# Splitting the first six W_in blocks of an encoder layer into four parts instead of two, and two swaps of order in its last layer norm

## The chip, the cores and the metric

The kernel is written for one core of a Trainium2 chip: TensorE (matrix products), VectorE, ScalarE, GpSimd and SyncE, each with its own queue of instructions, an on-chip memory of 128 partitions, and eight accumulator banks of 128 x 512 fp32. It runs as one program on one core. The metric is the device time of one execution in microseconds (us). In the profile the engines are PE (with PEld for its weight loads), DVE (VectorE), ACT (ScalarE), POOL (GpSimd) and SP (SyncE).

## The reference

One layer of an encoder over two groups of 256 tokens (512 in all), D = 1024, fp32:

```python
mod = (silu(c) @ w_mod + b_mod)                  # shift1, scale1, gate1, shift2, scale2, gate2 per group
h = layer_norm(x) * (1 + scale1) + shift1
z = h @ w_in + b_in                              # (1024, 5120): u | v | p | gates
a = gelu(u) * (w_spatial @ ln(gelu(v)) + b)      # in chunks of 128 tokens, 8 heads
b = pool_scale * W_g(mean_window(p) - p)         # windows 2, 4, 8, 16
t = (sig(g_a) * (a @ w_branch_a) + sig(g_b) * (b @ w_branch_b)) @ w_out
x = ln(alpha * x + gate1 * t)
h = layer_norm(x) * (1 + scale2) + shift2
f = moe(h)                                       # 1 of 4 groups, 2 of its 8 experts, SwiGLU, 32 experts in all
y = ln(alpha * x + gate2 * f)
```

## The kernel before

**Split products.** Most products of the first half are made of three fast ones: each operand is held as hi (rounded to fp32r) plus lo (the rest), and hi x hi, hi x lo and lo x hi are summed in a bank. ScalarE makes the hi copy of a weight tile (`w_hi`), VectorE the lo (`w_lo`); the same for h (`h_hi`, `h_lo`). A "block" is 128 columns of W_in for all 512 tokens: 8 chunks (of 128 rows of W_in) x 3 products of 128 x 512. There are 56 blocks; the first eight are the v columns. W_in comes in units of 512 columns (four blocks, 2 MB), double buffered in `raw`.

**The start (to about 65 us).** The six first blocks (`FIRST = 6`) can't begin with whole chunks, since h needs the modulation: shift1 and scale1 come from c times 2048 columns of `w_mod` (8 MB). The 8 chunks of h are therefore cut into two parts of four (`PART`), and the matching columns of `w_mod` are loaded and multiplied part by part. The order is written out by hand for each queue:

- SP loads x (two transfers of 1 MB), then for each part eight transfers of 512 KB of `w_mod` and the W_in rows of that part for units 0 and 1 (lines 449 to 464). Then come sixteen transfers of 1 MB of the later modulation (`load_mod(8 + k)`; the buffer has two places, and load m waits for `pe_mod >= m - 1`), with W_in unit 2 in front of k = 3 (`load_unit`, which waits until block 3's split is done).
- TensorE: three `keep_clock` products (their result is not used), a modulation unit, transposes of the normalised x (`n_columns`, tiles of 128 tokens), and so on in turn; then the transposes of the scales (`first_mod_columns`), two more `keep_clock`s, and `part_pair(0)`: blocks 0 and 1 over part 0. Blocks 2 to 5 over part 0 follow, with the modulation units of part 1 between them, then `part_pair(1)`, then the loop over n (line 845) with block n over part 1, the transposes of the finished block n - 1, the transposes of `w_spatial` at n = 5, and one of the later modulation units at n = 1, 3, 5, 6, 7 (`mod_unit_at`). Six banks hold the six blocks open between the parts.
- ScalarE copies the transposed x to `n_t`, makes `w_hi` of the split blocks (`part_split_hi`) and half of the chunks of `h_hi` straight from `n_t`; the other half is copied from `h32`, which VectorE (`H_VECTOR`) and POOL (`H_POOL`) make.
- VectorE normalises x, adds the bias of the modulation (`first_mod_rows`), makes the scales (`first_scales`), `w_lo`, its share of `h32`, and `h_lo`.
- POOL, when the last `h_lo` is done (`dve_hlo >= KC`), issues the loads of `w_spatial`, `w_pool`, `b_spatial`, the router weights and biases (lines 578 to 587). TensorE's transposes at n = 5 wait for three of them.

**The middle.** The rest of W_in, the pools and gates, the two branches, W_out, the first layer norm and the routing follow, one block after the other on TensorE. The 32 experts (192 MB of weights) are loaded from the end of block 56 on.

**The end.** For four tiles i of 128 tokens the last layer norm adds three terms: `second_added(i)` and `based(i)` on VectorE put alpha x and two expert rows together (in a pair of banks, with a sum for the mean), TensorE adds the rows of the last two experts (`last_rows`), `base_means` and `means` make the means, ScalarE sums the squares (`deviation(i)`), VectorE applies mean and gain (`centred_gain`), makes the inverse deviation (`inverse`), and the scaled rows go out through ScalarE and POOL (`scaled`, tiles 0 and 1) or VectorE (`scaled_bias`, tiles 2 and 3). Tile 3's first step is done in halves (`based_half`).

Of the kernel before, what the change touches and what calls it, by code (L numbers as in the profile page):

```python
# [36 lines left out]
PART = KC // 2  # L37
H_DIRECT = (0, 1, 4, 5)
H_VECTOR = (3, 0, 7, 4)
H_POOL = (2, 1, 6, 5)  # L40


def hybrid_encoder(nc, x_prompt, x_sample, c_prompt, c_sample, w_mod, b_mod, w_in, b_in, w_spatial,
# [12 lines left out]
    with ctx:  # L56
# [5 lines left out]
        def sem(name):  # L62
# [20 lines left out]
        modraw0 = [at(f"modraw0_{i}", [128, 2, 2, 512], f32, o)  # L83
                   for i, o in enumerate([2 * SLOT + 8 * K * j for j in range(4)] + [32 * K, 40 * K] + [SLOT + 32 * K, SLOT + 40 * K])]
# [42 lines left out]
        modrow_first = at("modrow_first", [128, 2, 512], f32, S0 + 9728 + 4096)  # L127
# [259 lines left out]
        def first_mod_source(part, kc):  # L387
            return w_mod[0, 128 * kc:128 * kc + 128, 0:2048].rearrange("p (v f n) -> p v f n", v=2, f=2)[:, :, part, :]

        def halves_of_chunks(tiles, turn):  # L390

            first = PART * (turn // 2 % 2)
            return tiles[turn % 2][:, first:first + PART, :]

# [163 lines left out]
        def _(pool):  # L558
# [4 lines left out]
            for v in range(2):  # L563
                for r in range(REQ):
                    pool.dma_start(modrow_first[64 * v + r:64 * v + r + 1, :, :],
                                   b_mod[0:1, 1024 * v:1024 * v + 1024].rearrange("a (f n) -> a f n", f=2)).then_inc(s_bmod, 16)
# [4 lines left out]
            for kc in H_POOL:  # L571
# [142 lines left out]
        def _(pe):  # L714
# [15 lines left out]
            def first_mod_unit(part, q):  # L730
                if part == 0:
                    pe.wait_ge(s_m0[q], 32)
                else:
                    pe.wait_ge(s_m0[4 + q // 2], 64)
                for k in range(2):
                    for v in range(2):
                        j = 2 * v + k
                        x = mm(MOD[32 * j:32 * j + 32, :], silu_c[:, 2 * q + k, :], modraw0[4 * part + q][:, k, v, :], start=(q == 0), stop=(q == 3))
                x.then_inc(pe_mod, 1)

            def first_mod_columns(part):
                pe.wait_ge(dve_row0, part + 1)
                for k in range(4):
# [3 lines left out]
            for _ in range(3):  # L747
                keep_clock(512)
            pe.wait_ge(act_pro, 1)

            def n_columns(i):
                pe.wait_ge(dve_n, i + 1)
                if i >= 2:
                    pe.wait_ge(act_nt, 2 * (i - 1))
                for kc in range(KC):
                    bank = B[2 * (i % 2) + kc // 4]
                    x = pe.transpose(bank[:, 128 * (kc % 4):128 * (kc % 4) + 128], xin[:, i, 128 * kc:128 * kc + 128], ident)
# [12 lines left out]
            pe.wait_ge(dve_pro, 1)  # L770
            first_mod_columns(0)
            keep_clock(512)
            keep_clock(256)

            def block_at(b, i, mov_hi, mov_lo, freed, count):
                pe.wait_ge(act_whi, FIRST + b + 1)
                pe.wait_ge(dve_wlo, FIRST + b + 1)
# [8 lines left out]
            def part_split(part, b):  # L786
                turn = FIRST * part + b
                pe.wait_ge(act_whi, turn + 1)
                pe.wait_ge(dve_wlo, turn + 1)
                return bank_of(b), halves_of_chunks(w_hi, turn), halves_of_chunks(w_lo, turn)  # L790

            def part_pair(part):
                for k in range(PART):
                    kc = PART * part + k
                    pe.wait_ge(act_hhi, kc + 1)
                    for b in range(2):
                        if k == 0:
                            part_split(part, b)
                        hi, lo = (halves_of_chunks(w, FIRST * part + b) for w in (w_hi, w_lo))
                        mm(bank_of(b)[:, :], hi[:, k, :], h_hi[:, kc, :], start=(kc == 0), stop=False)  # L800
                        mm(bank_of(b)[:, :], lo[:, k, :], h_hi[:, kc, :], start=False, stop=False)
                for k in range(PART):
                    kc = PART * part + k
                    pe.wait_ge(dve_hlo, kc + 1)
                    for b in range(2):
                        x = mm(bank_of(b)[:, :], halves_of_chunks(w_hi, FIRST * part + b)[:, k, :], h_lo[:, kc, :], start=False, stop=(kc == KC - 1))
                        if k == PART - 1:
                            x.then_inc(pe_blk if part else pe_part, 1)

            def part_block(part, b):  # L810
# [6 lines left out]
                x.then_inc(pe_blk if part else pe_part, 1)  # L817
# [27 lines left out]
            for n in range(8):  # L845
                if 2 <= n < FIRST:
                    part_block(1, n)
# [1696 lines left out]
```

## Time and profile before

| | |
|---|---|
| three runs | 943.0, 945.49, 944.63 us, median 944.63 |
| profiled execution | 942.63 us, its span 940.9 us |
| granted TensorE clock, mean | 0.991 |
| PE busy | 897.1 us (95%), 4420 products |
| DVE, ACT, POOL busy | 381.0, 243.1, 118.1 us |
| moved by DMA | 295.32 MB, mean 314 GB/s |

Busy times are sums over the span. A product's duration in the trace is longer than the step from one product to the next, since they are pipelined. A row of the timeline gives start, duration, engine, line and operation, the tiles written and read, how many instructions it merges, and in brackets the idle time in front of it with what ended it. Most products have line 716, that of a helper; they are told apart by their tiles (`modraw,silu_c` is a modulation unit, `cst` a keep_clock).

### The profile page before, as it was taken

Reading aid. Unit: us, or ns where it says so; the run is one execution under the profiler, and the core shown is the slowest. Engines: PE = TensorE matmul, PEld = TensorE weight load, DVE = VectorE, ACT = ScalarE, POOL = GpSimd, SP = SyncE. Lnnn points to the kernel's source line nnn. Section 1 sums busy time; section 2 is a strip of 40 time slices with the busy share of each in tenths; the row PEclk is TensorE's granted clock in tenths of the full one; section 3 lists DMA queues with packets and bytes.
Section 4 is the critical chain, followed back from the end, with each engine's and each line's share of the span. In section 5 each row is a group of like instructions: output and inputs, shape, how many; then the busy total and the mean of one; then the engine's idle time right before and its main releaser. Section 6 shows DMA issues by size and latency. Waiting matters only on the chain. (4 is left out here: it accounts for less than half of the span.)

```text
span 940.9 us, 12139 instructions
## 1 busy us (share of the span) xinstructions
PE 897.1 (95%) x4420; PEld 547.3 (58%) x4420; DVE 381.0 (40%) x657; ACT 243.1 (26%) x360; POOL 118.1 (13%) x149
## 2 busy tenths in 40 slices
PE   5999999999999999999999999998998999999894
PEld 2677767888888888787544444444444344444331
DVE  5543434565344236798622322222122132321346
ACT  3342335331333225446410111011011101110113
POOL 3130556000001000000000000000000100000041
PEclk9999999999999999999999999999999999999997
DMA  9975676274665623908999999999999999999993
GB/s 341 363 246 191 224 269 224 90 267 179 222 225 153 183 90 101 300 1 367 399 384 419 427 426 426 426 427 427 429 426 425 424 387 428 429 427 427 422 412 122
DMA packets 51291, 295.32 MB, mean 314 GB/s; under 512 B 5438, under 2 KB 6558, under 8 KB 35986
## 3 DMA queue, kind: packets, MB, share of 16 engines
q1 hardware_dynamic: 40784, 263.47, 69.9%
q0 software_dynamic: 9952, 29.80, 9.4%
q10 hardware_dynamic: 482, 1.13, 0.3%
q8 instruction: 39, 0.64, 0.3%
q14 instruction: 34, 0.28, 0.1%
HBM read 275.81 MB, written 22.83 MB: 317 GB/s over the span
## 5 line engine op out<-in xcount | busy, mean ns | idle before, releaser
L716 PE MATMUL banks<-down_w,hid_t 128*64 128x512 f32 x512 | 119.7, 610 | 11.9 <-issue 10.9
L716 PE MATMUL banks<-h_hi,w_hi 128*128 128x512 f32 x320 | 125.0, 391 | 0.5 <-ACT h_hi L1398 0.5
L716 PE MATMUL banks<-h_lo,w_hi 128*128 128x512 f32 x320 | 125.2, 398 | 0.0
L716 PE MATMUL banks<-h_hi,w_lo 128*128 128x512 f32 x320 | 124.8, 390 | 0.0
L716 PE MATMUL banks<-up_w,x_by_expert 128*64 128x512 f32 x256 | 112.6, 593 | 0.0
L716 PE MATMUL banks<-gate_w,x_by_expert 128*64 128x512 f32 x256 | 112.5, 592 | 0.0
L716 PE MATMUL banks<-up_w,x_by_pair 128*64 128x512 f32 x240 | 105.4, 592 | 0.0
L716 PE MATMUL banks<-gate_w,x_by_pair 128*64 128x512 f32 x240 | 105.4, 592 | 0.0
L1615 ACT ACTIVATE sg_hid<-banks 64x512 f32<-64x512 f32 x33 | 19.5, 592 | 313.8 <-PE banks L716 313.8
L2177 DVE TENSOR_TENSOR sg_hid<-banks,sg_hid 64x512 f32<-64x512 f32 x32 | 22.2, 694 | 177.9 <-ACT sg_hid L1615 177.9
L685 POOL DMA_INDIRECT round_y<-yout,store_row x30 | 31.0, 1034 | 461.5 <-DVE yout L2300 448.7
L1806 DVE TENSOR_TENSOR w_lo<-raw,w_hi 128x1024 fp32r<-128x1024 f32 x50 | 61.4, 1228 | 67.0 <-ACT w_hi L1353 66.9
L716 PEld LDWEIGHTS banks<-down_w,hid_t 128*64 128x64 f32 x512 | 36.3, 140 | 72.2 <-issue 65.2
L716 PEld LDWEIGHTS banks<-gate_w,x_by_expert 128*64 128x64 f32 x256 | 34.9, 137 | 70.8 <-issue 70.7
L1353 ACT ACTIVATE w_hi<-raw 128x1024 fp32r<-128x1024 f32 (+1 forms) x62 | 59.8, 970 | 61.2 <-PE banks L716 54.3
L716 PEld LDWEIGHTS banks<-h_lo,w_hi 128*128 128x128 f32 x320 | 60.1, 188 | 25.1 <-issue 8.4
L716 PEld LDWEIGHTS banks<-gate_w,x_by_pair 128*64 128x64 f32 x240 | 32.9, 137 | 66.5 <-issue 66.5
L716 PE MATMUL banks<-sel_group,h_hi 128*128 128x256 f32 x256 | 69.7, 306 | 0.0
L2300 DVE TENSOR_TENSOR yout<-banks,yout 128x512 f32<-128x512 f32 x32 | 22.1, 691 | 112.9 <-PE banks L716 112.8
L716 PEld LDWEIGHTS banks<-h_hi,w_hi 128*128 128x128 f32 x320 | 60.2, 188 | 12.7 <-ACT h_hi L1398 1.1
L716 PEld LDWEIGHTS banks<-h_hi,w_lo 128*128 128x128 f32 x320 | 60.1, 188 | 12.7
L716 PE MATMUL banks<-sel_group,h_lo 128*128 128x256 f32 x256 | 63.6, 282 | 1.4 <-issue 1.4
(331 smaller groups left out, 1314.7 us busy)
## 6 DMA issues: line engine op xcount, KB each, us to landing
down_w<-in_w_exp_down SPq DMA_DIRECT2D x29, 2048.0 KB, 20.5
gate_w<-in_w_exp_gate SPq DMA_DIRECT2D x28, 2048.0 KB, 18.5
up_w<-in_w_exp_up SPq DMA_DIRECT2D x28, 2048.0 KB, 22.9
modraw<-in_w_mod SPq DMA_DIRECT2D x16, 1024.0 KB, 4.9
raw<-in_w_in SPq DMA_DIRECT2D x8, 2048.0 KB, 9.7
round_y<-zrow POOLq DMA_DIRECT2D x6, 2048.0 KB, 7.6
modraw<-in_w_mod SPq DMA_DIRECT2D x16, 512.0 KB, 11.4
down_w<-in_w_exp_down SPq DMA_DIRECT2D x6, 1024.0 KB, 14.8
```

What stands on the lines that cost most here:

```text
L685: pool.indirect_dma_start(round_halves, bass.IndirectOffsetOnAxis(store_row[:, e:e + 1], 0), yout[s][:, :], None, bounds_check=2 * LAST_RO ...
L716: return pe.matmul(out, lhsT, rhs, start=start, stop=stop, skip_group_check=True)
L1353: return act.activation(out, in_, ACT.Copy, scale=scale)
L1615: act.activation(sgb[0:CAP, :], bank[0:CAP, :], ACT.Silu).then_inc(sm["silu"], 1)
L1806: dve.tensor_tensor(w_lo[par][:, :, :], raw[:, u % 2, :, 128 * (b % 4):128 * (b % 4) + 128], w_hi[par][:, :, :].bitcast(f32), ALU.subtract ...
L2177: dve.tensor_tensor(sg_hid[CAP:128, :], B[0][CAP:128, :], sg_hid[0:CAP, :], ALU.mult).then_inc(m_sem["hid"], 1)
L2300: dve.tensor_tensor(yout[s][:, :], B[1][:, :], yout[s][:, :], ALU.mult).then_inc(m_sem["yo"], 1)
```

## The change

**Start.** The parts are four of two chunks. A part needs 256 columns of shift and of scale, so its eight modulation transfers are of 256 KB (pieces of 1 KB) instead of 512 KB; there are 32 instead of 16. The W_in rows of a part are two chunks. Of unit 1 only half the columns are loaded with part 0, the others behind part 1. TensorE has one `keep_clock` of 512 columns at first and one of 256 behind the first two modulation units; those around the first scales go. The transposes of x are done in halves: the first four chunks of all tiles ahead of the first scales, the last four of tiles 1 to 3 between the scales' transposes and the first products, and ScalarE copies their results between the splits of part 0. All of `h_hi` comes straight from `n_t` on ScalarE; VectorE makes the even chunks of `h32`, POOL the odd. The loads of the later modulation wait for all eight units of the first (`pe_mod >= 8`).

**End.** VectorE does tile 3's add ahead of the means, ScalarE tile 2's squares ahead of tile 0's scaled rows.

The core of the diff:

```diff
-PART = KC // 2
-H_DIRECT = (0, 1, 4, 5)
-H_VECTOR = (3, 0, 7, 4)
-H_POOL = (2, 1, 6, 5)
+NPART = 4
+PART = KC // NPART
+WIDE = 128 * PART
+BEFORE = FIRST * (NPART - 1)
...
 # SP
-                    sp.wait_ge(dve_wlo, FIRST + 4 * (u - 1))
+                    sp.wait_ge(dve_wlo, BEFORE + 4 * (u - 1))
...
-                sp.wait_ge(pe_mod, m - 1)
+                sp.wait_ge(pe_mod, max(KC, m - 1))
...
-            for part in range(2):
+            for part in range(NPART):
                 for kc in range(KC):
-                    m = 4 * part + kc // 2
-                    landed = s_m0[4 + kc // 4 if part else kc // 2]
-                    sp.dma_start(modraw0[m][:, kc % 2, :, :], first_mod_source(part, kc)).then_inc(landed, 16)
+                    landed = s_m0[part + 1 if part else kc // 4]
+                    sp.dma_start(modraw0[part][kc // 2][:, kc % 2, :, :], first_mod_source(part, kc)).then_inc(landed, 16)
                 chunks = slice(PART * part, PART * part + PART)
                 if part == 0:
                     for c in range(2):
                         cols = slice(256 * c, 256 * c + 256)
                         sp.dma_start(raw[:, 0, chunks, cols], unit_source(0)[:, chunks, cols]).then_inc(s_wpre[c], 16)
-                    sp.dma_start(raw[:, 1, chunks, :], unit_source(1)[:, chunks, :]).then_inc(s_wpre[2], 16)
+                    sp.dma_start(raw[:, 1, chunks, 0:256], unit_source(1)[:, chunks, 0:256]).then_inc(s_wpre[1], 16)
                 else:
                     for u in range(2):
-                        sp.dma_start(raw[:, u, chunks, :], unit_source(u)[:, chunks, :]).then_inc(s_w[u], 16)
+                        landed = {1: s_m0[5], 2: s_wpre[2], 3: s_w[u]}[part]
+                        sp.dma_start(raw[:, u, chunks, :], unit_source(u)[:, chunks, :]).then_inc(landed, 16)
+                if part == 1:
+                    sp.dma_start(raw[:, 1, 0:PART, 256:512], unit_source(1)[:, 0:PART, 256:512]).then_inc(s_m0[5], 16)
...
 # TensorE
-            for _ in range(3):
-                keep_clock(512)
+            keep_clock(512)
             pe.wait_ge(act_pro, 1)
...
-            first_mod_unit(0, 0)
-            n_columns(0)
-            n_columns(1)
-            first_mod_unit(0, 1)
-            n_columns(2)
-            n_columns(3)
-            first_mod_unit(0, 2)
-            first_mod_unit(0, 3)
+            first_mod_units(0, 0, 2)
             keep_clock(256)
-            pe.wait_ge(act_nt, 2 * TILES)
+            n_columns(0, 0)
+            n_columns(0, 1)
+            n_columns(1, 0)
+            first_mod_units(0, 2, 4)
+            n_columns(2, 0)
+            n_columns(3, 0)
             pe.wait_ge(dve_pro, 1)
             first_mod_columns(0)
-            keep_clock(512)
-            keep_clock(256)
+            for i in range(1, TILES):
+                n_columns(i, 1)
...
-            part_pair(0)
-            first_mod_unit(1, 0)
-            part_block(0, 2)
-            first_mod_unit(1, 1)
-            part_block(0, 3)
-            first_mod_unit(1, 2)
-            first_mod_unit(1, 3)
-            part_block(0, 4)
-            pe.wait_ge(dve_col, 1)
-            first_mod_columns(1)
-            part_block(0, 5)
-            part_pair(1)
+            for part in range(NPART - 1):
+                part_pair(part)
+                part_block(part, 2)
+                first_mod_units(part + 1, 0, 4)
+                part_block(part, 3)
+                first_mod_columns(part + 1)
+                part_block(part, 4)
+                part_block(part, 5)
+            part_pair(NPART - 1)
             for n in range(8):
                 if 2 <= n < FIRST:
-                    part_block(1, n)
+                    part_block(NPART - 1, n)
...
 # ScalarE
             for i in range(TILES):
...
+                n_copied(i, 0)
             part_split_hi(0, 0)
             part_split_hi(0, 1)
+            act.wait_ge(act_nt, TILES)
             h_high(0)
-            for b in range(2, FIRST):
-                part_split_hi(0, b)
-            part_split_hi(1, 0)
-            part_split_hi(1, 1)
-            h_high(1)
+            part_split_hi(0, 2)
+            n_copied(0, 1)
+            n_copied(1, 1)
+            part_split_hi(0, 3)
+            n_copied(2, 1)
+            n_copied(3, 1)
+            part_split_hi(0, 4)
+            part_split_hi(0, 5)
+            act.wait_ge(act_nt, 2 * TILES)
+            for part in range(1, NPART):
+                part_split_hi(part, 0)
+                part_split_hi(part, 1)
+                h_high(part)
+                if part < NPART - 1:
+                    for b in range(2, FIRST):
+                        part_split_hi(part, b)
...
             deviation(1)
+            deviation(2)
             scaled(0)
-            deviation(2)
             scaled(1)
...
 # VectorE
+            for part in range(NPART):
+                first_mod_rows(part)
+                part_split_lo(part, 0)
+                if part:
+                    part_split_lo(part, 1)
+                first_scales(part)
+                dve.wait_ge(dve_col, 2 * part + 2)
+                if part == 0:
+                    part_split_lo(part, 1)
+                elif part == 2:
+                    dve.wait_ge(act_nt, 2 * TILES)
+                modulated(PART * part)
+                for kc in range(PART * part, PART * part + PART):
+                    h_low(kc)
+                if part < NPART - 1:
+                    for b in range(2, FIRST):
+                        part_split_lo(part, b)
...
             based(2)
+            second_added(3)
             base_means(0, 3)
             means()
-            second_added(3)
             dve.wait_ge(f_open, 3)
```

`first_mod_units(part, first, last)` does the units first to last of a part with 256 columns each (four products a unit, on four strips of 32 columns of the array), and `n_columns(i, hb)` four transposes of tile i instead of eight.

## Rows read from the trace of the kernel before

**Rows 1.** Windows by stage: busy us (instructions) per engine, granted clock, DMA share, GB/s.

```profile
100.00:200.00 100.00, 99.70 (x469) 74.07 (x462) 46.02 (x65) 44.13 (x62) 38.69 (x49) 1.00 0.57 208
400.00:920.00 520.00, 502.34 (x2565) 245.56 (x2563) 178.08 (x366) 91.26 (x156) 41.97 (x42) 0.99 0.95 398
```

**Rows 2.** Timeline of TensorE at the start (start, duration in us): keep_clock products.

```profile
10.37 5.49 PE L716 MATMUL banks<-cst 128*128 128x512 f32 x6
...
25.20 1.46 PE L716 MATMUL banks<-cst 128*128 128x512 f32 x4
```

**Rows 3.** The same timeline, from the first product of the blocks on.

```profile
27.16 0.50 PE L716 MATMUL banks<-h_hi,w_hi 128*128 128x512 f32 x1 [0.51 <-ACT h_hi L1398]
...
40.47 0.39 PE L716 MATMUL banks<-h_hi,w_lo 128*128 128x512 f32 x1
40.78 1.92 PE L716 MATMUL banks<-modraw,silu_c 128*32 128x512 f32 x16
...
42.98 0.40 PE L716 MATMUL banks<-h_hi,w_hi 128*128 128x512 f32 x1
...
52.36 1.98 PE L716 MATMUL banks<-h_lo,w_hi 128*128 128x512 f32 x8
54.89 0.66 PE L825 MATMUL banks<-cst,g 128*128 128x128 f32 x4 [0.55 <-ACT g L1432]
```

**Rows 4.** Timeline of the POOL and SP queues, 50 to 80 us: loads issued.

```profile
51.90 0.99 POOL L579 DMA_DIRECT2D ws_raw<-in_w_spatial  x1 [2.64 <-DVE h_lo L1840]
...
56.60 0.33 SPq L447 DMA_DIRECT2D modraw<-in_w_mod  x1
...
64.20 15.90 SPq L447 DMA_DIRECT2D modraw<-in_w_mod  x3
```

**Rows 5.** DMA issues at 56.60 and 64.20: KB, us to landing.

```profile
modraw<-in_w_mod SPq DMA_DIRECT2D x1, 1024.0 KB, 11.3
...
modraw<-in_w_mod SPq DMA_DIRECT2D x1, 1024.0 KB, 12.2
```

**Rows 6.** Timeline of VectorE at the end.

```profile
921.13 0.16 DVE L2425 SCALAR_TENSOR_TENSOR fin<-banks,fin 128x4 f32<-128x4 f32 x1 [1.08 <-PE banks L716]
921.21 1.28 DVE L2322 SCALAR_TENSOR_TENSOR y_second<-y_second,route_w,res 128x1024 f32<-128x1024 f32 x1
...
923.66 1.28 DVE L2445 SCALAR_TENSOR_TENSOR y_first<-banks,fin,ln_bc 128x1024 f32<-128x1024 f32 x1
...
929.08 1.29 DVE L2445 SCALAR_TENSOR_TENSOR banks<-banks,fin,ln_bc 128x1024 f32<-128x1024 f32 x1 [0.59 <-ACT squares L1720]
```

**Rows 7.** Timeline of the SP queue, the first loads.

```profile
1.89 9.28 SPq L455 DMA_DIRECT2D modraw<-in_w_mod  x8
11.22 4.05 SPq L460 DMA_DIRECT2D raw<-in_w_in  x2
```

**Rows 8.** DMA issue at 1.89 (KB, us to landing), and the window 20 to 21.

```profile
modraw<-in_w_mod SPq DMA_DIRECT2D x1, 512.0 KB, 9.4
...
20.00:21.00 1.00, 1.00 (x10) 1.00 (x11) 0.00 (x0) 0.23 (x1) 0.00 (x0) 1.00 1.09 353
```

**Rows 9.** Timeline of TensorE, transposes of w_spatial and modulation unit 3.

```profile
70.57 1.04 PE L855 MATMUL banks<-cst,ws_raw 128*128 128x128 f32 x8
...
78.64 1.06 PE L716 MATMUL banks<-modraw,silu_c 128*32 128x512 f32 x8
```

**Rows 10.** Timeline of ScalarE at the start.

```profile
18.16 2.06 ACT L1353 ACTIVATE n_t<-banks 128x512 f32<-128x512 f32 x4 [5.16 <-PE banks L757]
...
26.02 2.08 ACT L1398 ACTIVATE h_hi<-n_t,mod_t,scale1p 128x256 fp32r<-128x256 f32 x4 [1.86 <-DVE scale1p L1825]
```

**Rows 11.** Timeline of ScalarE at the end.

```profile
926.71 1.15 ACT L1353 ACTIVATE y_second<-y_first,fin 128x1024 f32<-128x1024 f32 x1 [1.43 <-DVE fin L2454]
927.77 1.09 ACT L1720 ACTIVATE squares<-banks,fin 128x1024 f32<-128x1024 f32 x1
```

**Rows 12.** Timeline of TensorE at the end.

```profile
922.51 2.85 PE L716 MATMUL banks<-yout,last_t 64*128 64x512 f32 x12
```

More of the change, by code:

```diff
@@ L387, in first_mod_source, with part_of_chunks @@
         def first_mod_source(part, kc):
-            return w_mod[0, 128 * kc:128 * kc + 128, 0:2048].rearrange("p (v f n) -> p v f n", v=2, f=2)[:, :, part, :]
-        def halves_of_chunks(tiles, turn):
-            first = PART * (turn // 2 % 2)
+            return w_mod[0, 128 * kc:128 * kc + 128, 0:2048].rearrange("p (v f n) -> p v f n", v=2, f=NPART)[:, :, part, :]
+        def part_of_chunks(tiles, turn):
+            first = PART * (turn // 2 % NPART)
             return tiles[turn % 2][:, first:first + PART, :]
@@ L728, in keep_clock, with first_mod_units @@
                 mm(B[4][:, 0:w], ident, cst[:, 0:w])
-            def first_mod_unit(part, q):
+            def first_mod_units(part, first, last):
                 if part == 0:
-                    pe.wait_ge(s_m0[q], 32)
+                    pe.wait_ge(s_m0[first // 2], 64)
                 else:
[L734 to L739, printed above, removed]
+                    pe.wait_ge(s_m0[part + 1], 128)
+                for q in range(first, last):
+                    for k in range(2):
+                        for v in range(2):
+                            j = 2 * v + k
+                            x = mm(MOD[32 * j:32 * j + 32, 0:WIDE], silu_c[:, 2 * q + k, :], modraw0[part][q][:, k, v, :], start=(q == 0), stop=(q == 3))
+                    if q % 2 == 1:
+                        x.then_inc(pe_mod, 1)
@@ L762, in _, with n_columns @@
-            n_columns(1)
-            first_mod_unit(0, 1)
-            n_columns(2)
-            n_columns(3)
-            first_mod_unit(0, 2)
-            first_mod_unit(0, 3)
-            keep_clock(256)
-            pe.wait_ge(act_nt, 2 * TILES)
+            def n_columns(i, hb):
+                bank = B[i if hb == 0 else (4, 5, 0, 1)[i]]
+                if hb == 0:
+                    pe.wait_ge(dve_n, i + 1)
+                elif i >= 2:
+                    pe.wait_ge(act_nt, i - 1)
+                for k in range(4):
+                    first = 512 * hb + 128 * k
+                    x = pe.transpose(bank[:, 128 * k:128 * k + 128], xin[:, i, first:first + 128], ident)
+                x.then_inc(pe_xt, 1)
@@ L805, in part_pair @@
                     for b in range(2):
-                        x = mm(bank_of(b)[:, :], halves_of_chunks(w_hi, FIRST * part + b)[:, k, :], h_lo[:, kc, :], start=False, stop=(kc == KC - 1))
+                        x = mm(bank_of(b)[:, :], part_of_chunks(w_hi, FIRST * part + b)[:, k, :], h_lo[:, kc, :], start=False, stop=(kc == KC - 1))
                         if k == PART - 1:
-                            x.then_inc(pe_blk if part else pe_part, 1)
+                            x.then_inc(pe_blk if part == NPART - 1 else pe_part, 1)
             def part_block(part, b):
@@ L816, in part_block @@
                     x = mm(bank[:, :], lo[:, k, :], h_hi[:, kc, :], start=False, stop=(kc == KC - 1))
-                x.then_inc(pe_blk if part else pe_part, 1)
+                x.then_inc(pe_blk if part == NPART - 1 else pe_part, 1)
             def transposes(k, zs, trs):
@@ new lines, in n_copied, with h_high @@
+            def n_copied(i, hb):
+                act.wait_ge(pe_xt, ((1, 3, 4, 5), (2, 6, 7, 8))[hb][i])
+                copy(n_t[:, 4 * hb:4 * hb + 4, 128 * i:128 * i + 128],
+                     B[i if hb == 0 else (4, 5, 0, 1)[i]][:, :].rearrange("p (k n) -> p k n", k=4)).then_inc(act_nt, 1)
+            def h_high(part):
+                act.wait_ge(dve_col, 2 * part + 2)
+                for kc in range(PART * part, PART * part + PART):
+                    for r in range(REQ):
+                        x = act.activation(h_hi[:, kc, SEQ * r:SEQ * r + SEQ], n_t[:, kc, SEQ * r:SEQ * r + SEQ], ACT.Identity,
+                                           scale=scale1p[:, kc, r:r + 1], bias=mod_t[:, 0, kc, r:r + 1])
+                    x.then_inc(act_hhi, 1)
```

115 lines of the change are left out of this document (37 added, 78 removed).

## The prediction

> **What bounds the kernel now.** I read the busy time by stage first: in 100 to 200 us TensorE works 99.70 of 100 us, and the experts' stage (400 to 920 us) runs at a DMA share of 0.95 from loads that start only when the last W_in block is done [rows 1]. So any time won or lost before 100 us, if it is not given back there, comes out at the end. Then I read TensorE's own timeline of the start: 27.16 us pass before the first product of real work, which waits for ScalarE's h_hi, and from there products follow each other nearly without a gap to 54.34, where the second pair ends, and after 0.55 us of waiting for the first GELU on through the blocks [rows 2, 3]. Last, the transfers: the loads that the later steps of this stage wait for are issued by SP and POOL when TensorE and VectorE reach certain points [rows 4, 5]. At the end VectorE is the chain: it stands idle 1.08 us before the means and 0.59 us before tile 2's gain [rows 6].
>
> The profiled execution took 942.63 us (span 940.9, 1.7 around it); the median of the runs shown is 944.63. I work out a difference on the profile and put it on the median.
>
> **When the first product starts.** The first 512 KB of modulation weights landed 9.4 us after their issue at 1.89, at 11.3 [rows 7, 8]. While 1 KB pieces passed (the two half loads of the first W_in unit) the queues moved 353 GB/s [rows 8]. 512 KB are 1.5 us at that rate, so the weights of a part begin to land at about 9.8; the first half of part 0 (1.05 MB) is there at 12.8, the second at 15.8, where the old part 0 needed 4.2 MB, to about 21.7. TensorE: one keep_clock of 512 columns instead of three, two records of 0.915 [rows 2], ends at 12.2. Two mod units, 256 columns wide: 1.7 us at that pace, 0.9 at the later one (three 512-column equivalents in 1.46, so 0.49 a record [rows 2]). Then keep_clock(256), 12 transposes at 0.13 (8 took 1.04 [rows 9]) or twice that, two units, 8 transposes. At the full pace from 15.5 on this ends at 18.9, at half pace throughout at 22.0. ScalarE then has one more n_t copy (4 took 2.06 [rows 10]), a split of 256 columns (about 0.35), VectorE its own (0.4) and the scales (0.6), ScalarE the first h_hi (two of 0.52 [rows 10]): 3.1 us. First product at 22.0 or 25.2. The pace changed somewhere between 15.9 and 25.2 before [rows 2]; I take 23.0, **4.2 us earlier** than 27.16. The 12 transposes of the second n_t halves (1.6 us) lie in front of the pair, but beside the scales and h_hi, so they cost nothing.
>
> **What the four parts cost on TensorE.** A product follows the last by 0.227 us (eight took 1.98, the last lasting 0.39 [rows 3]). Two 512-column mod units cost 42.98 - 40.47 - 2 x 0.227 = 2.06 us [rows 3]; four 256-column units have the same columns. Two transposes of scales: 0.26. A part is 36 products, the units and the transposes of the next: 8.17 + 2.06 + 0.26 = 10.5 us. Three parts and the last pair (12 products, 2.72): the pair ends 34.5 us after the first product, at 57.5 instead of 54.34. Behind it 24 products are left instead of 48, 5.46 us less. TensorE alone would thus be at mod unit 3 (the fourth of the later ones, in block 6) at 57.5 + (78.64 - 54.34) - 5.46 = 76.3, against 78.64 [rows 9]: **2.3 us won**. The 4.2 won at the start pay 1.9 for two more sets of units and transposes and shorter waits.
>
> The other engines keep up: in part 0 ScalarE has six splits (2.1), h_hi (2.1) and four n_t copies (2.1) for 10.5 us of products; each later part less. All of part 3's modulation weights have landed at 9.8 us + 11.55 MB / 353 GB/s = 42.5 (four times 2.10 MB, the W_in pieces of the first three parts 3.15), and are needed 25.2 after the first product, at 48.2. The waits added (act_nt before the banks of part 0, pe_part before a w place is used again) are for things done at least 2 us before; queued behind them is only the same block.
>
> **What is late next.** Mod units 2 and 3 of the later modulation need loads that can't be issued earlier: load 10 waits for unit 0, which stands behind the last pair; W_in unit 2 waits for block 3's split; load 11 stands behind it on SP. POOL's eight loads wait for the last h_lo. All of them come later, not earlier, because the last pair ends later: the last scales are transposed 28.6 us after the first product, and 1.1 for the scales, 2.1 for two chunks of h_hi and 0.7 for h_lo put h_lo's end at 55.5 instead of 51.6 (+3.9; POOL's first issue was 51.90 [rows 4]), load 10 from 56.60 to 59.8 (+3.2). And they are slow there: load 10 took 11.3 us, load 11 12.2, for 1 MB each [rows 5], and the queues are full from POOL's first load on. Load 11 landed at 64.20 + 12.2 = 76.4, 2.2 before its unit at 78.64 [rows 4, 5, 9]. Now its unit would be ready at 76.3, and the load lands 3.2 to 3.9 later than before: I take 3.4, 79.8. The stall is 3.5 us, spread over units 2 and 3, and unit 3 starts **1.2 us later** than before (bounds: 2.3 earlier with no stall, 1.7 later with the full 3.9). From there the loads and needs are as before. That is where the expected gain goes.
>
> **The tail.** Tile 3's add (1.28 us at 921.21) fills the 1.08 us idle ahead of the means [rows 6]; the means go 0.3 later, to 921.4. TensorE is busy until 922.08 anyhow. The next half product of tile 3 then starts a microsecond earlier, but tile 0's gain waits for the squares of tile 0, which follow the means (end 922.9 instead of 922.5): from 923.66 to 922.9, 0.75 us won. On ScalarE tile 2's squares ran at 927.77, behind the scaled rows of tile 0 at 926.71 [rows 11], though TensorE had finished tile 2 at 922.51 + 2.85 = 925.36 [rows 12]. Moved ahead they run at 925.4 and are through at 926.9, just as the scaled rows become ready. VectorE's 0.59 us of waiting before 929.08 goes too: 929.08 - 0.59 - 0.75 = 927.75. What follows is one chain on VectorE to the end; tile 3's squares come at 929.1, in time. **1.25 us won** (0.7 if the squares still come last, 1.4 at most). POOL's adds of tiles 0 and 1 go at most 0.3 later, and end 1.3 before tile 3's rows.
>
> **Sum:** +1.2 - 1.25 = 0: 942.6 by the profile, 944.6 on the median.
>
> **Rivals.**
> A. The loads keep up (POOL's loads, with the queues free of load 10 a little longer, end sooner): no stall, 2.3 + 1.25 = 3.55 won, 941.1. For it: the 2.2 us of slack that load 11 had. Against: the queues were full then, and both triggers move later. Chance 0.18.
> B. TensorE's pace stays at half through the start, since two keep_clocks ahead of it and two behind go and 1 us of idle comes in at 12.2: first product at 25.2, everything in the stage 2.2 later, +2.1: 946.7. For it: the six records of 0.915 at 10.37 [rows 2], where steady work had not yet raised the pace. Against: from 12.8 on the work is close to gapless, and before, with TensorE at work since 10, the granted clock was 1.00 (the upper level, 2.4 GHz) at 20 to 21 [rows 8]. Chance 0.14. The Trainium skill (TensorE: Matmul & The Clock Gate, Part 1) says that the slow clock is the default and that activity releases it; by that rule what matters is how gapless the new start is, and by it the 25.2 would be the upper end. The pace in [rows 2] agrees with two levels a factor of two apart.
> C. The slower one: 1 KB pieces pass at the pace of their issue, 2.0 us for 512 KB in the first W_in unit, 262 GB/s [rows 7]. Place: the modulation weights of the parts. Of the 11.55 MB 9.45 are in 1 KB pieces, so part 3's land at 9.8 + 9.45 / 0.262 + 2.1 / 0.353 = 51.8, TensorE waits at each part, the last pair ends at 51.8 + 9.3 = 61.1 (+6.7), load 11 lands at 83.1: +4.5 - 1.25 = +3.3, 947.9. It decides from about 290 GB/s down, and from 270 it is slower by more than 0.3%. Against it: the 353 GB/s while such pieces moved. Chance 0.10. [...]
>
> **Chances.** My forecast 0.55, A 0.18, B 0.14, C 0.10, else 0.03. A measurement of this kernel tells about 0.3% (2.8 us) from no change. Faster: A and a little of the forecast, 0.22. Slower: C and the upper part of B, 0.16. Same 0.62. Range 940.8 to 948.0: A at the one end, C at the other.
>
> **What would show it.** First product at 22 to 24 us; the last pair of the split blocks ending near 57; two DMA waits on TensorE, before mod units 2 and 3, of some 3.5 us together, and unit 3 at 79 to 80. No idle on VectorE before tile 2's gain, and the tail shorter by about 1.2. Wrong if unit 3 runs near 76 with no wait (A), if the first product comes after 25 (B), or if TensorE waits for modulation weights inside the parts (C).

## The result, and the profile after

The changed kernel takes 948.83 us (median of 20 runs, 944.7 to 952.54) against 944.68 (20 runs, 942.05 to 946.11) for the kernel before beside it: ratio 1.0047, 95% interval 1.0035 to 1.0058. It is slower by 4.2 us. The prediction had 944.6, no difference, and a range that ended at 948.0. The profiled execution spans 944.9 us against 940.9.

TensorE's timeline of the start in the changed kernel (start and duration in us, what it did, the idle time just ahead):

```profile
13.40 1.94 PE L719 MATMUL banks<-modraw,silu_c 128*32 128x256 f32 x16 [0.96 <-DMA modraw<-in_w_mod]
...
23.33 0.50 PE L719 MATMUL banks<-h_hi,w_hi 128*128 128x512 f32 x1 [1.63 <-ACT h_hi L1405]
...
27.71 1.93 PE L719 MATMUL banks<-modraw,silu_c 128*32 128x256 f32 x32
...
38.23 1.93 PE L719 MATMUL banks<-modraw,silu_c 128*32 128x256 f32 x32
...
48.74 1.93 PE L719 MATMUL banks<-modraw,silu_c 128*32 128x256 f32 x32
...
58.51 0.66 PE L834 MATMUL banks<-cst,g 128*128 128x128 f32 x4 [0.55 <-ACT g L1447]
```

The first product of real work comes 3.8 us earlier than before (27.16 in [rows 3]), the parts follow each other in 10.5 us without a wait for weights, and the transposes behind the last pair come at 58.51 instead of 54.89. All of this is as predicted, within 0.5 us. The size of the gain differs between profiles: the first product comes at 26.16 to 27.24 us in the four profiles with the start of before (before, e1, e13, e14) and at 23.13 to 24.48 in the eight whose start up to there is that of the changed kernel. Then the same engine, further on: the transposes of w_spatial, mod units 2 and 3 with the products behind unit 3, and unit 4 (units are counted from 0; load 8 + k feeds unit k):

```profile
69.52 1.09 PE L861 MATMUL banks<-cst,ws_raw 128*128 128x128 f32 x8 [0.67 <-DMA bs_bc<-in_b_spatial]
71.50 1.06 PE L719 MATMUL banks<-modraw,silu_c 128*32 128x512 f32 x8 [0.89 <-DMA modraw<-in_w_mod]
...
81.62 1.70 PE L719 MATMUL banks<-modraw,silu_c 128*32 128x512 f32 x8 [2.94 <-DMA modraw<-in_w_mod]
83.25 0.80 PE L719 MATMUL banks<-h_lo,w_hi 128*128 128x512 f32 x1
83.84 0.63 PE L719 MATMUL banks<-h_hi,w_hi 128*128 128x512 f32 x1
...
90.31 1.06 PE L719 MATMUL banks<-modraw,silu_c 128*32 128x512 f32 x8
```

Three waits for transfers, 4.50 us together, where [rows 9] had none; and the unit behind the longest takes 1.70 us instead of 1.06, the products 0.63 instead of 0.39. The windows there (busy time of PE, PEld, DVE, ACT, POOL; granted clock; DMA share; GB/s) show the clock at its lower level, 0.50, that is 1.2 GHz, after 2.9 us in which TensorE stood still, though it was busy throughout those 2 us:

```profile
82.00:84.00 2.00, 2.00 (x10) 0.66 (x3) 0.00 (x0) 0.00 (x0) 0.00 (x0) 0.50 0.21 86
84.00:86.00 2.00, 2.00 (x8) 1.59 (x7) 0.00 (x0) 0.00 (x0) 0.00 (x0) 0.67 0.81 209
```

From mod unit 3 to mod unit 4 it takes 8.69 us; before, 85.74 - 78.64 = 7.10. Unit 3 is 3.0 us later than before, unit 4 4.57. The loads behind it, on the queues of GpSimd and SyncE and as transfers (KB, us to landing; the two transfers are loads 10 and 11):

```profile
56.30 0.99 POOL L582 DMA_DIRECT2D ws_raw<-in_w_spatial  x1 [1.85 <-DVE h_lo L1852]
...
60.22 0.33 SPq L448 DMA_DIRECT2D modraw<-in_w_mod  x1
60.59 0.62 SPq L444 DMA_DIRECT2D raw<-in_w_in  x1
65.07 0.33 SPq L448 DMA_DIRECT2D modraw<-in_w_mod  x1
...
modraw<-in_w_mod SPq DMA_DIRECT2D x1, 1024.0 KB, 11.2
...
modraw<-in_w_mod SPq DMA_DIRECT2D x1, 1024.0 KB, 16.5
```

Load 11 is issued 0.9 us later than in [rows 4] but takes 16.5 us instead of 12.2 [rows 5]. From there on little is given back: the stages of [rows 1] read nearly the same,

```profile
100.00:200.00 100.00, 99.87 (x471) 74.04 (x470) 43.41 (x59) 41.00 (x58) 39.02 (x51) 1.00 0.58 208
400.00:920.00 520.00, 504.99 (x2569) 248.27 (x2569) 176.39 (x368) 92.83 (x156) 42.25 (x42) 0.99 0.95 396
```

the first expert's gate weights are issued at 384.96 instead of 380.43 (+4.53), and expert 31's down product starts at 917.96 instead of 913.87 (+4.09). The end is measured from there. VectorE's timeline answers to [rows 6], SyncE's shows the output stores:

```profile
925.44 0.16 DVE L2434 SCALAR_TENSOR_TENSOR fin<-banks,fin 128x4 f32<-128x4 f32 x1
...
931.87 1.28 DVE L2454 SCALAR_TENSOR_TENSOR banks<-banks,fin,ln_bc 128x1024 f32<-128x1024 f32 x1
...
937.27 1.28 DVE L2468 SCALAR_TENSOR_TENSOR y_second<-banks,fin,ln_bc 128x1024 f32<-128x1024 f32 x1
...
934.64 0.56 SPq L554 DMA_DIRECT2D out<-y_second  x1
935.24 0.58 SPq L556 DMA_DIRECT2D out<-y_second  x1
935.87 4.19 SPq L554 DMA_DIRECT2D out<-y_second  x3
```

Both idle times of [rows 6] are gone, and VectorE is through 20.59 us after 917.96, where before it was 21.70 after 913.87: 1.1 won. But the span ends 26.94 after it, before 27.03: 0.1 won. Behind VectorE's last instruction 6.35 us pass instead of 5.33. Tile 3's store on SyncE's queue, before and then in the changed kernel, makes up most of that: it starts 0.03 us behind VectorE's end before, 0.19 now, and takes 1.32 us to issue instead of 0.47.

```profile
935.60 0.47 SPq L551 DMA_DIRECT2D out<-y_second  x1
```

```profile
938.74 1.32 SPq L554 DMA_DIRECT2D out<-y_second  x1
```

### The profile page after: what moved, and what is told of

Same layout as the page of the kernel before. It is cut to its first block and busy times, and to the rows that moved or that the text cites. A ratio compares the mean times of both kernels' runs of the same rounds, so it can differ in the third digit from the quotient of the medians.

```text
span 944.9 us, 12332 instructions
## 1 busy us (share of the span) xinstructions
PE 897.2 (95%) x4476; PEld 549.2 (58%) x4476; DVE 382.4 (40%) x677; ACT 246.7 (26%) x376; POOL 118.3 (13%) x149
## 5 line engine op out<-in xcount | busy, mean ns | idle before, releaser
L719 PE MATMUL banks<-down_w,hid_t 128*64 128x512 f32 x512 | 122.0, 620 | 10.8 <-issue 8.9
L719 PEld LDWEIGHTS banks<-h_lo,w_hi 128*128 128x128 f32 x320 | 60.3, 189 | 24.5 <-issue 10.3
## 6 DMA issues: line engine op xcount, KB each, us to landing
down_w<-in_w_exp_down SPq DMA_DIRECT2D x6, 1024.0 KB, 10.8
```

The source lines that it names most:

```text
L719: return pe.matmul(out, lhsT, rhs, start=start, stop=stop, skip_group_check=True)
```

## The experiments

**Theory**: the parts do what they should; the loss is the late loads of 56 to 82 us, the lower clock behind the wait, and output stores that crowd. **Rivals**: the parts themselves cost it, the waits only show it; or the exchanges at the end do. Read from each profile are the first real product, mod unit 4 (a mark behind all the start's waits), VectorE's end and the span's end behind the start of expert 31's down product, and the median with its ratio to the kernel before on the same chip. Each mark is read from one profile; the medians are of 5 to 20 runs, but e5 and e8 were run once and have no ratio. The kernel before took 942.99 to 944.68 us in these groups; e1, e13 and e14 have its start, e2 and e8 that of the changed kernel.

| kernel | first product | mod unit 4 | VectorE's end | span's end | median us | ratio (95%) |
|---|---|---|---|---|---|---|
| before | 27.16 | 85.74 | 21.70 | 27.03 | 944.68 | 1 |
| changed | 23.33 | 90.31 | 20.59 | 26.94 | 948.83 | 1.0047 (1.0035-1.0058) |
| e1 tail alone | 26.16 | 85.64 | 20.06 | 27.06 | 944.13 | 1.0005 (0.9989-1.0020) |
| e2 start alone | 24.41 | 91.57 | 21.90 | 26.68 | 948.38 | 1.0048 (1.0033-1.0064) |
| e3 load 11 first | 24.26 | 88.71 | 20.69 | 27.21 | 944.97 | 1.0008 (0.9990-1.0026) |
| e4 third place | 24.48 | 87.14 | 21.71 | 28.41 | 944.22 | 0.9995 (0.9979-1.0012) |
| e5 busy through the wait | 23.13 | 88.81 | 20.29 | 26.95 | 946.76 | one run |
| e6 + ws, wp, bs early | 24.10 | 85.51 | 20.59 | 26.80 | 944.10 | 1.0004 (0.9989-1.0020) |
| e7 + product at the start | 22.33 | 83.15 | 20.84 | 27.14 | 942.25 | 0.9986 (0.9971-1.0001) |
| e12 (e7 again) | 21.98 | 82.63 | 21.56 | 28.28 | 942.33 | 0.9982 (0.9963-1.0000) |
| e11 (e7, add alone) | 22.29 | 83.06 | 20.97 | 25.91 | 939.36 | 0.9955 (0.9937-0.9974) |
| e8 fewer stores | 23.14 | 88.58 | 21.83 | 26.91 | 946.43 | one run |
| e9 ws, wp, bs early alone | 24.06 | 86.34 | 21.41 | 28.16 | 944.13 | 1.0002 (0.9979-1.0026) |
| e10 (e9 + product) | 22.77 | 86.08 | 20.63 | 27.07 | 942.39 | 0.9979 (0.9960-0.9998) |
| e13 before + add | 27.24 | 85.83 | 20.76 | 26.19 | 942.61 | 0.9979 (0.9964-0.9994) |
| e14 before + squares | 27.05 | 85.67 | 21.02 | 27.61 | 944.02 | 0.9994 (0.9978-1.0010) |

**e1, e2: each half of the change alone.** e1 is the kernel before with the two exchanges at the end (the last hunk under ScalarE and the last under VectorE), e2 the changed kernel without them.

> The kernel before with the two exchanges at the end alone (tile 3's add ahead of the means, tile 2's squares ahead of tile 0's scaled rows). Theory (the loads of the start and the output stores decide): VectorE's last instruction ends about 20.6 us after main_down(31) instead of 21.7, but the last two output stores then stand behind the others, so the time moves by -0.3 to +0.2 us: about 944.6. As the prediction had it: -1.25 us, 943.4. Rival (the tail itself costs, since tile 0's rows are scaled later): slower by 0.5 us or more, 945.2 or above.

> The changed kernel with the old order at the end: the four parts alone. Theory: the whole loss is the start's, so about +4.1 us on before (948.8), and the mod unit 4 of the first loop still starts 4.6 us later than before (90.3 against 85.74). Rival (part of the loss is the tail's): 948.0 or less. If the prediction's tail gain of 1.25 us had been real at the end: 950.

The whole loss is the start's: e2's interval (five runs) is nearly that of the changed kernel, e1's takes in 1. VectorE ends earlier in e1, and the span's end does not move.

**e3: load 11 ahead of W_in unit 2.**

```diff
-                if k in (3, 8, 12):
-                    load_unit(k // 4 + (2 if k == 3 else 1))
+                if k in (8, 12):
+                    load_unit(k // 4 + 1)
                 load_mod(8 + k)
+                if k == 3:
+                    load_unit(2)
```

> The changed kernel, with W_mod's load 11 issued ahead of the 2 MB load of W_in unit 2 on SyncE's queue, nothing else. Theory (mod unit 3 waits for load 11, which shares the transfer engines with unit 2 and with GpSimd's loads): load 11 is issued at about 65 us as now, but lands at 75 to 77 instead of 81.6; the wait of 2.94 us before mod unit 3 goes, the unit takes 1.06 instead of 1.70 us, the products after it keep 0.23 us spacing, and mod unit 4 starts at 85.8 instead of 90.3: about -4.5 us, 944.3. W_in unit 2 lands at 80 to 84, before block 8 wants it. Rival (the parts themselves cost it: the blocks' work of part 3 ends 3.6 us later, and the wait only shows it): another wait takes its place, mod unit 4 stays at 89 or later, 947.5 or more.

The wait before unit 3 is gone, load 11 taking 10.6 us instead of 16.5, and the ratio falls from 1.0047 to 1.0008: by the time the rival falls. By the mark it is close: mod unit 4 comes at 88.71, where 85.8 was expected and the rival had 89 or later. The first product is 0.9 later, and another wait costs clock: behind 0.84 us for bs and 1.16 for load 10, 2 us apart, unit 2 takes 1.50 us, the window behind it shows

```profile
74.00:76.00 2.00, 2.00 (x8) 1.41 (x5) 0.00 (x0) 0.00 (x0) 0.00 (x0) 0.50 1.02 377
```

and unit 3 follows in 8.72 us instead of 7.1.

**e4: a third place for the loads of W_mod.** It keeps e3's order of load 11 and W_in unit 2.

```diff
-        modraw = at("modraw", [128, 2, 4, 512], f32, SLOT + 32 * K)
+        modraw = [at(f"modraw{j}", [128, 4, 512], f32, o) for j, o in enumerate((SLOT + 32 * K, SLOT + 40 * K, 20 * K))]
...
-            for k in range(16):
+            for k in (2, 0, 1, *range(3, 16)):
```

> The changed kernel with a third place in SBUF for W_mod's loads: load 10 needs no place of an earlier one and is issued ahead of loads 8 and 9, into the 5 us in which the transfer engines now stand still (46 to 51 us); load 11 takes load 8's place (issued at about 60 instead of 65 us) and goes ahead of W_in unit 2. Theory: no wait for W_mod is left (0.89 and 2.94 us gone), perhaps 0.3 to 0.7 us for GpSimd's last load remains; mod unit 4 starts at 84.2 to 85 us instead of 90.3 (before: 85.74): -5.4 to -6.1 us on the changed kernel, 942.8 to 943.4, 1 to 2 us under the kernel before. Rival (the parts themselves cost it): not under 946.

The stretch that it is to fill, in the changed kernel (DMA share and GB/s at the end of the line):

```profile
46.00:51.00 5.00, 5.00 (x47) 3.29 (x46) 1.08 (x4) 0.54 (x2) 0.00 (x0) 1.00 0.00 0
```

No wait for loads 10 and 11 is left, and the ratio is 0.9995. The 942.8 to 943.4 us expected did not come (944.22), nor did unit 4 at 84.2 to 85 (87.14): the first product is 1.15 later than in the changed kernel, and bs, which GpSimd issues last of its large loads, is now what TensorE waits for, 1.89 us instead of the 0.3 to 0.7 expected:

```profile
71.88 1.09 PE L869 MATMUL banks<-cst,ws_raw 128*128 128x128 f32 x8 [1.89 <-DMA bs_bc<-in_b_spatial]
```

**e5: TensorE kept busy through the wait.** Its one run took 946.76 us.

```diff
+                if n == 6:
+                    for _ in range(3):
+                        mm(COL[:, 0:512], ident, cst[:, 0:512])
```

> The changed kernel with three more 128x512 products of the identity into a free bank just ahead of mod unit 3, where TensorE now waits 2.94 us (some 2.2 us of work at the full level). Theory (the wait itself is the load's, but behind it TensorE runs at 1.2 GHz for some 3.5 us because it stood still, and this costs 1.6 us more): unit 3 starts no earlier against the first product, the unit takes 1.06 us, the products behind it keep 0.23 us spacing, and the distance from mod unit 3 to mod unit 4 is 7.1 us instead of 8.69. Rival (the slow products after the wait have another cause, as the arriving transfers): the distance stays at 8.7 us, or grows.

```profile
77.80 2.74 PE L719 MATMUL banks<-cst 128*128 128x512 f32 x6
81.70 1.06 PE L719 MATMUL banks<-modraw,silu_c 128*32 128x512 f32 x8 [1.16 <-DMA modraw<-in_w_mod]
...
88.81 1.06 PE L719 MATMUL banks<-modraw,silu_c 128*32 128x512 f32 x8
```

The wait ends at the same time, the load being no earlier, but unit 4 follows in 7.11 us: 1.6 us of the loss were the clock's, paid behind the wait and not in it. e8, which has the changed kernel's start unaltered, shows the same by chance: there bs was late, TensorE waited 2.62 us for it and only 0.50 for load 11, the clock fell at the first of the two (0.50 at 72 to 74 us), and from unit 3 to unit 4 it took 7.10.

**e6, e9: GpSimd's loads earlier**, on the third place (e6) and alone on the changed kernel (e9).

```diff
             for kc in range(1, KC, 2):
+                if kc == KC - 1:
+                    pool.wait_ge(dve_hlo, 3 * PART)
+                    pool.dma_start(ws_raw[:, :, :], ...)
+                    ...
```

> The kernel with a third place for W_mod's loads, and GpSimd's loads of ws, wp and bs issued ahead of its last modulated block, behind h_lo of part 2 (at about 45.5 us instead of 56.3), so that they move in the 5 us in which the transfer engines stand still. Theory: the wait of 1.89 us for bs before the transposes of ws goes, no wait of TensorE for a transfer is left between 56 and 90 us; mod unit 4 starts 60.7 us behind the first real product (62.7 without this step, 67.0 in the changed kernel): about -1.9 us against the third place alone, 942.3, some 1.5 us under the kernel before. Rival (these loads only collide with load 10 and loads 8 and 9 instead): mod unit 0 or 1 waits, and the time stays at 944 or more.

> The changed kernel with GpSimd's loads of ws, wp and bs (2 MB) issued behind h_lo of part 2, at about 45.5 us, and nothing else: two places for W_mod's loads and their order as in the changed kernel. Theory (the late loads are late because five transfers share the engines after 56 us): load 10, W_in unit 2 and load 11 have the engines nearly to themselves, 4 MB from 60.2 us at the 400 GB/s that the profile shows is 10.5 us, so load 11 is there by 71 to 73, and no wait for it or for bs is left; mod unit 4 starts 60.7 to 61.5 us behind the first real product (67.0 in the changed kernel): about 943 to 944, the same as with the third place as well. Rival (it is the late issue of load 11 and unit 2 ahead of it that matter, not GpSimd's loads): a wait of 1.5 us or more before mod unit 3 stays, 946 or more.

bs is no longer waited for in either, and in e9 nothing waits before units 1 to 4, with the two places and the order of the changed kernel. So what made load 11 late was GpSimd's 2 MB and the 2 MB of W_in unit 2 together: taking either out of its way is enough (e9, e3). What these loads now run into is what e6's rival said and the two theories missed: loads 8 and 9 took a median of 10.8 us in e6 and 11.4 in e9, against 5.8 in the changed kernel, mod unit 0 waits 0.76 and 1.65 us, and e6 took 944.10 us where its theory had 942.3. On the whole time e6 and e9 are no better than e4.

**e7, e10, e12: one more product at the start**, `keep_clock(256)` behind `keep_clock(512)`; e7 and e12 are one kernel, on e6, e10 is on e9.

> The kernel of the run before with one more 128x256 product of the identity ahead of the first mod unit, into the 0.9 to 1.3 us in which TensorE waits for W_mod's first pieces. Theory (that idle microsecond puts off the step to 2.4 GHz, which came at about 16 us in one profile of the changed start and at 18 to 19 in three others, with the first real product at 23.3 and 24.3 to 24.5): the step comes by 15 us, and the first real product starts at 22.0 to 23.3: -1.0 to -2.4 us, about 941. Rival (the first product hangs on the transfers or on ScalarE's rows, not on TensorE's level): it stays at 23.3 or later, the time as the run before.

> The run before (loads of ws, wp and bs earlier) with one more 128x256 product of the identity ahead of the first mod unit. Theory: first real product at 22.3 us as in the run with the third place and this product, the time about 942, no different from that run's; the third place is then not needed. Rival: mod unit 2 or 3 waits for its load by 1 us or more, since TensorE gets there 1 to 2 us earlier; 943.5 or more.

> The kernel with the third place, the earlier loads and the one more product at the start, once more, beside the kernels that it is to be compared with. Expected as the first time: 942.3 us, 0.1 to 0.2% under the kernel before, mod unit 4 at 83.2 to 84 us.

```profile
10.44 2.93 PE L728 MATMUL banks<-cst 128*128 128x512 f32 x4
13.31 1.53 PE L728 MATMUL banks<-modraw,silu_c 128*32 128x256 f32 x16
14.78 0.70 PE L728 MATMUL banks<-cst 128*128 128x256 f32 x2
15.31 1.47 PE L776 MATMUL banks<-cst,xin 128*128 128x128 f32 x12
```

This is e12. The mod units at 13.31 are already faster than the 1.94 of the changed kernel, the 12 transposes take 1.47 us where e2, e3, e4, e6 and e9 show 2.54 to 2.77, and the first real product comes at 21.98 to 22.77 in all four profiles with the extra product, against 23.13 to 24.48 in the eight profiles without it; the granted clock rises at 13.8 to 16.0 us in the four and at 16.5 to 19.4 in the eight. With it and the third place the start is at last ahead of before: mod unit 4 at 82.6 to 83.2 instead of 85.74. In e10, without the third place, unit 0 waits 1.15 us (0.05 to 0.21 in e7, e11 and e12), the clock falls (0.56 at 62 to 64 us), and unit 4 comes at 86.08, though the time of the whole can't be told from e7's. The fall does not follow from the length of the wait: e9 waited 1.65 us at the same place and kept the clock. Units 0 and 1 in e10, then in e9:

```profile
59.73 1.36 PE L720 MATMUL banks<-modraw,silu_c 128*32 128x512 f32 x8 [1.15 <-DMA modraw<-in_w_mod]
...
66.13 1.07 PE L720 MATMUL banks<-modraw,silu_c 128*32 128x512 f32 x8
```

```profile
61.54 1.07 PE L720 MATMUL banks<-modraw,silu_c 128*32 128x512 f32 x8 [1.65 <-DMA modraw<-in_w_mod]
...
66.38 1.06 PE L720 MATMUL banks<-modraw,silu_c 128*32 128x512 f32 x8
```

**e8: fewer stores.** Its one run took 946.43 us.

> The changed kernel, which leaves out the two output stores of tile 1 (that quarter of the output is not written), so that nothing is queued between the stores of tile 2 and tile 3. Theory (the 1.1 us that VectorE wins at the end are lost because the stores crowd): the stores of tile 3 are issued in 0.5 us instead of 1.32, and the span ends 5.3 us or less behind VectorE's last instruction instead of 6.35. Rival (the end hangs on tile 3's own stores, whatever else is stored): it stays 6.2 to 6.5 us.

The span ends 5.08 us after VectorE's last instruction: the theory's 5.3 or less. Tile 3's store is issued in 0.51 us, as expected:

```profile
939.65 0.51 SPq L554 DMA_DIRECT2D out<-y_second  x1
```

The table's 26.91 behind expert 31's down product seems to show no gain, but here that mark moves: see e11.

**e11, e13, e14: the two exchanges apart.** e11 is e7 without the exchange of the squares; e13 and e14 are the kernel before with one exchange each.

> The kernel with the third place, the earlier loads and the one more product at the start, with only one of the two exchanges at the end: tile 3's add stays ahead of the means, tile 0's scaled rows go ahead of tile 2's squares again. Theory (the end hangs on the output stores, and tile 0's go first): tile 0's stores are issued 0.5 us or more earlier against main_down(31), tile 2's 0.5 to 1 us later, and the span ends 26.5 to 27.0 us behind main_down(31), as in the kernel before (27.03) and the changed kernel (26.94): no difference in time, 942. Rival (the exchange of the squares is what keeps the add's gain from showing): the span ends 26.2 us or less behind it, 941.3.

> The kernel before with tile 3's add ahead of the means, nothing else. Theory (the add's gain is real, and the exchange of the squares gave it away): tile 0's scaled rows start some 0.8 us earlier behind main_down(31), VectorE's last instruction ends 21.0 us behind it instead of 21.70, the stores stay as spread out as before, and the span ends 25.9 to 26.2 us behind it instead of 27.03: -0.8 to -1.1 us. Rival (the stores hide any gain of VectorE): 26.7 to 27.1 us behind it, no difference.

> The kernel before with tile 2's squares ahead of tile 0's scaled rows, nothing else. Theory: tile 0's and tile 1's stores are issued 0.5 to 1.1 us later, VectorE's last instruction ends 0 to 0.4 us earlier, and the span ends 27.0 to 28.0 us behind main_down(31) instead of 27.03: 0 to +1 us. Rival (the squares are what the prediction took them for, a gain on the way to tile 3): 26.6 us or less behind it.

e11's rival was right, and the theory that the stores hide any gain fell with it: with the add alone the span ends 25.91 us (e11) and 26.19 (e13) behind expert 31's down product, with both exchanges 26.80 to 28.41 in ten profiles, with the squares alone 27.61. Part of this spread is the mark's own. In e4, e8, e9 and e12 the granted clock has just fallen to 0.50 when that product starts, and its 16 parts take 4.8 to 5.3 us instead of 3.65; the changed kernel, then e12:

```profile
917.96 3.65 PE L719 MATMUL banks<-down_w,hid_t 128*64 128x512 f32 x16
```

```profile
912.72 4.98 PE L728 MATMUL banks<-down_w,hid_t 128*64 128x512 f32 x16
```

Counted from the first product behind it instead (`yout,last_t`), the span ends after 22.6 to 22.9 us in all ten profiles with both exchanges, 22.8 and 22.4 with neither (before, e2), 21.6 and 21.9 with the add alone (e11, e13), 23.4 with the squares alone (e14), and 21.0 in e8, without tile 1's stores. SyncE's stores of e11, and how long each takes to issue (min/median/max in ns) in e11 and in the changed kernel:

```profile
927.27 0.56 SPq L562 DMA_DIRECT2D out<-y_second  x1
927.87 0.58 SPq L564 DMA_DIRECT2D out<-y_second  x1
929.49 3.67 SPq L562 DMA_DIRECT2D out<-y_second  x3
...
L562 SPq DMA_DIRECT2D out<-y_second x4: 466/514/602, 927.3 to 932.7; - x4
```

```profile
L554 SPq DMA_DIRECT2D out<-y_second x4: 560/966/1754, 934.6 to 938.7; - x4
```

Tile 0's first store leaves 927.27 - 911.69 = 15.6 us behind the down product in e11, 934.64 - 917.96 = 16.7 in the changed kernel, 930.39 - 913.87 = 16.5 before. The squares put ahead hold up tile 0's and tile 1's scaled rows; tile 2's stores then come in the same microseconds, and tile 1's and tile 3's take 1.75 and 1.32 us to issue, in e11 0.60 and 0.47. Why a store takes longer to issue there is not shown; e8 shows that it is the other stores that do it. e11 is the version that beats both: its interval lies under 1 and, at a ratio of 0.9955 against 1.0047, under the changed kernel (those of e10 and e13, both 0.9979, lie just under 1 as well). Its tail explains 1.1 us of its lead over e12 (942.33 to 939.36), counted from the first product behind the down product; the rest is not explained, and the intervals of the two overlap.

## Why the prediction was wrong

- **The start** held: first product at 23.33 (23.0 said), a part in 10.5 us (10.5), transposes behind the pair at 58.51 (pair's end 57.5 plus the first GELU's 0.55; the terms given for the 34.5 us from the first product to the pair's end add to 34.2, and 34.6 were measured). Without the waits unit 3 would have run at 81.62 - 4.50 = 77.1 (76.3 said). Rivals B and C did not happen in the form given: the pace was full from the second mod units (18.07) on, and the 1 KB pieces kept up. But B's cause is real: in e2, e3, e4, e6 and e9 the clock rose 1.5 to 2.3 us later than in the changed kernel's profile (at 18.5 to 19.4 instead of 17.1), first product at 24.1 to 24.5. The Trainium skill (TensorE: Matmul & The Clock Gate, Part 1) says that the number of slow products at a start differs from run to run for one kernel; the eight profiles of this start agree, the clock rising at 16.5 to 19.4 us.
- **"The stall is 3.5 us, ... unit 3 starts 1.2 us later" is the step that failed**, in size. The mechanism, later triggers for loads 10, unit 2 and 11, was right, and so was the issue of load 10 (60.22, 59.8 said). The landing of load 11 was not: it was put 3.4 us later than before, at 79.8, and came 5.2 later, at 81.6. Its issue moved by only 0.9 us, since mod unit 1, which triggers it, came only 0.9 later. But the prediction gave it its old 12.2 us, where it took 16.5: GpSimd's loads, issued 4.4 us later than before (56.30 for 51.90), and unit 2 were still moving beside it. The two errors in part cancelled. The waits came to 4.50 us, one of them, 0.67 for bs, not foreseen, and unit 3 to 3.0 later.
- **The clock behind the wait was not in the sum.** It cost 1.6 us more (8.69 instead of 7.10 to the next unit; e5 gives it back). 1.2 + 1.8 + 1.6 = 4.6, the 4.57 measured at unit 4, and all but 0.4 of it is in the medians, as said of any time lost before 100 us. The 4.57 is one profile's: with the same start unit 4 comes 5.8 later than before in e2 and 2.8 later in e8.
- **The tail's 1.25 us** were priced at VectorE's end, where 1.1 came, and not at the span's end, where 0.1 did. I had followed POOL's adds but not the stores behind them. The add alone is worth 0.8 to 1.1 us at the end against the kernel before (e13, e11), 0.5 to 0.8 against e2; the exchange of the squares takes it back. This term, 1.25 in the sum and 0.1 at the end, is the second that failed.

## What to carry to other kernels

Work moved ahead of a stretch must be followed to the transfers that are triggered by its end: a load that comes 1 us later can land 5 us later where others now overlap with it, and the price of a wait includes the slow products behind it. Find the stretch in which the transfer engines stand still (here 46 to 51 us) and see what can be loaded in it; here that brought the time back to that of the kernel before and no further (e4, e6 and e9 have ratios of 0.9995 to 1.0004), the loads moved into it delaying others in e6 and e9. At the end of a kernel the last store's landing is the mark, not the last instruction: an order that makes every tile ready at once can lose what it won.

## What was not expected of the hardware

- The length of a wait does not tell whether it costs clock. The granted clock fell to 0.50 behind waits of 2.94, 3.54 (e2) and 2.62 us (e8), but also behind one of 1.15 (e10: from unit 0 to unit 1 6.40 us instead of e9's 4.84) and behind 0.84 and 1.16 us 2 us apart (e3). Waits of 1.65 (e9) and 1.89 us (e4: from unit 2 to unit 3 7.12) cost none. What decides between them is not shown.
- The experts' stage, with a DMA share of 0.95, differs between runs: from the first expert's load to expert 31's down product it took 532.4 to 537.8 us in the sixteen profiles. A start that is 2 us better is seen in one profile by its marks, and in the time only over many runs.
- Loads 8 and 9 (1 MB each, issued together) took a median of 5.8 us with the engines otherwise free; beside GpSimd's 2 MB SyncE's loads of 1 MB took 8.4 (e12) to 16.5 us, the slowest with W_in unit 2 ahead of them. Stores of 256 KB were issued in some 0.5 to 0.6 us each when spread out (e11) and in up to 2.0 when crowded (e12).
